# Loading and splitting x by token tiles with whole rows, instead of by column pieces, in a one-core decoder-layer kernel

## The reference, cut to what matters

```python
def _rmsnorm(x, g):
    xf = x.astype(jnp.float32)
    xf = xf * lax.rsqrt(jnp.mean(xf * xf, axis=-1, keepdims=True) + EPS)
    return xf.astype(x.dtype) * g
...
    xn = _rmsnorm(x, n1g)
    z = xn @ w_in
    bg, cg, xt, q, k, v, o, ig, fg = jnp.split(z, _SPLIT_IDX, axis=-1)
```

## Time and profile before

| what | value |
|---|---|
| median of 3 runs | 2495.88 us (2492.79 to 2497.23) |
| the profiled execution's own time | 2492.38 us |
| its span in the profile | 2490.3 us |
| TensorE busy | 2458.9 us (99%) |
| DVE busy | 1771.7 us (71%) |
| ACT busy | 895.0 us (36%) |
| mean granted TensorE clock | 0.997 of full speed |

### The profile page before, as it was taken

How to read it: one execution, slowest core, us unless ns; L and a number is a source line. 1 busy time by engine, 2 the same in 40 slices (tenths; PEclk the granted TensorE clock), 3 DMA queues, 4 the chain that set the end, 5 groups by cost and what they waited for, 6 DMA issues and landing times.

```text
span 2490.3 us, 44310 instructions
## 1 busy us (share of the span) xinstructions
PE 2458.9 (99%) x17632; PEld 2393.4 (96%) x17632; DVE 1771.7 (71%) x2487; ACT 895.0 (36%) x1236; POOL 38.4 (2%) x60
## 2 busy tenths in 40 slices
PE   8999999999999998999999999999999999999998
PEld 8999999999999997999999999999999899999886
DVE  7576575575687668887778777877777866866435
ACT  5212222222133335434343434343444533544313
POOL 0000000000000000000000000000000000000100
PEclk9999999999999999999999999999999999999999
DMA  5433333333235665344343433434333655745722
GB/s 131 99 119 95 84 112 100 89 104 102 86 115 155 186 200 187 111 127 119 102 134 111 128 112 109 127 110 128 100 111 105 250 155 158 266 129 142 274 81 76
DMA packets 458922, 325.54 MB, mean 131 GB/s; under 512 B 14130, under 2 KB 429006, under 8 KB 456368
## 3 DMA queue, kind: packets, MB, share of 16 engines
q1 hardware_dynamic: 403704, 250.29, 34.6%
q10 hardware_dynamic: 51448, 58.42, 7.7%
q0 software_dynamic: 3584, 14.16, 1.5%
HBM read 264.49 MB, written 58.34 MB: 130 GB/s over the span
## 4 chain that ended last, share of the span: by engine, by line
PE 94%; DVE 3%; DMA 2%; ACT 1%; issue 1%; SPq 0%; DVEq 0%; ACTq 0%
PE ps L604 21%; PE ps L844 17%; PE ps L848 17%; PE ps L846 17%; PE ps L607 10%; PE ps L612 3%; PE ps L859 2%; PE ps L952 2%; PE ps L956 2%; PE ps L954 2%; DMA xtok<-in_x_sample_dram 1%; DMA opraw<-hop 0%; PE ps L960 0%; PE ps L961 0%; PE ps L871 0%
## 5 line engine op out<-in xcount | busy, mean ns | idle before, releaser
L844 PE MATMUL ps<-ophi,gw_ring 128*128 128x288 f32 x3248 | 963.2, 297 | 11.7 <-ACT p1c L1291 6.6
L846 PE MATMUL ps<-oplo,gw_ring 128*128 128x288 f32 x3248 | 959.1, 295 | 0.0
L848 PE MATMUL ps<-ophi,gw_ring 128*128 128x288 f32 x3248 | 957.2, 295 | 0.0
L844 PEld LDWEIGHTS ps<-ophi,gw_ring 128*128 128x128 f32 x3248 | 610.1, 188 | 13.6 <-ACT p1c L1291 7.0
L848 PEld LDWEIGHTS ps<-ophi,gw_ring 128*128 128x128 f32 x3248 | 612.7, 189 | 0.0
L846 PEld LDWEIGHTS ps<-oplo,gw_ring 128*128 128x128 f32 x3248 | 610.9, 188 | 0.2
L1017 ACT ACTIVATE whi<-wraw 128x512 fp32r<-128x512 f32 x256 | 160.7, 632 | 597.3 <-PE ps L607 418.5
L604 PE MATMUL ps<-xhi,whi 128*128 128x288 f32 x1536 | 332.6, 298 | 0.0
L607 PE MATMUL ps<-xhi,wlo 128*128 128x288 f32 x1536 | 328.8, 296 | 0.0
L604 PE MATMUL ps<-xlo,whi 128*128 128x288 f32 x1536 | 328.7, 296 | 0.0
L2100 DVE TENSOR_TENSOR gw_ring<-graw_a,gw_ring 128x1024 fp32r<-128x1024 f32 x195 | 238.7, 1224 | 113.4 <-ACT gw_ring L1264 112.8
(11 more groups left out here) (338 smaller groups left out, 2667.6 us busy)
## 6 DMA issues: line engine op xcount, KB each, us to landing
wraw<-in_w_in_dram SPq DMA_DIRECT2D x96, 512.0 KB, 3.9
graw_a<-in_w_ffn_gate_dram SPq DMA_DIRECT2D x59, 512.0 KB, 3.8
graw_a<-in_w_ffn_up_dram SPq DMA_DIRECT2D x59, 512.0 KB, 4.7
graw_a<-in_w_ffn_down_dram SPq DMA_DIRECT2D x42, 512.0 KB, 6.3
wraw<-in_w_out_dram SPq DMA_DIRECT2D x32, 512.0 KB, 4.3
opraw<-hop SPq DMA_DIRECT2D x14, 1152.0 KB, 11.4
graw_b<-in_w_ffn_gate_dram SPq DMA_DIRECT2D x29, 512.0 KB, 3.8
graw_b<-in_w_ffn_up_dram SPq DMA_DIRECT2D x29, 512.0 KB, 4.8
```

The costliest lines, as they stand in the source:

```text
L844: pe.matmul(out, gw_ring[:, slot, 0, k, :], ophi[p][:, k, :], start=start and k == 0, stop=False, skip_group_check=True)
L846: pe.matmul(out, gw_ring[:, slot, 0, k, :], oplo[p][:, k, :], start=False, stop=False, skip_group_check=True)
L848: mm = pe.matmul(out, gw_ring[:, slot, 1, k, :], ophi[p][:, k, :], start=False, stop=k == GK - 1, skip_group_check=True)
```

## The change

SP loads x by token tiles: five DMAs of 96 whole rows of 8 KB, and two for the last tile. TensorE, ACT and DVE go by 12 units (token tile t, half of the columns), each with eight transposes and 128 x 768 elements. The gate products run by halves of the tokens: the first 32 matmuls stand behind the transposes of unit 8, the other 32 behind the last unit. The first two weight quarters are split after units 5 and 7. The squares are whole rows (2048 columns), three token tiles on ACT and three on DVE, after the last unit. There are fewer idle transposes, `gw_lo` counts what `gw_g` counted, and POOL clears `qz` after the squares are summed.

```diff
@@ -97,12 +97,11 @@
     K_FULL = (4, 4, 4, 4)
     assert sum(K_FULL) == KT
     MIX_K = tuple(range(NG, KT)) + tuple(range(NG))
-    X_PIECES = ((0, 2), (2, 2), (4, 4), (8, 4), (12, 4))
+    XU = 2 * XT
+    KU = KT // 2
     SMALLS = 10
-    SQ_ACT = 4
-    IDLE_FIRST, IDLE_X, IDLE_PIECE = 6, 14, (2, 8)
-    X_LAST = {k0 + n - 1: b for b, (k0, n) in enumerate(X_PIECES)}
-    assert sum(n for _, n in X_PIECES) == KT
+    SQ_ACT = 3
+    IDLE_FIRST, IDLE_X = 6, 10
     QS = float(DK) ** -0.5
     GK = KT // 2
     GU = 6
...
@@ -390,12 +389,10 @@
             xp = x_prompt.rearrange("l t d -> (l t) d")
             xs = x_sample.rearrange("b t d -> (b t) d")
             last = TP - (XT - 1) * XTW
-            for b, (k0, n) in enumerate(X_PIECES):
-                c = slice(k0 * P, (k0 + n) * P)
-                sp.dma_start(xtok[:, 0:XT - 1, c],
-                             xp[0:TP - last, c].rearrange("(t p) d -> p t d", p=XTW)).then_inc(tok_in[b], 16)
-                sp.dma_start(xtok[0:last, XT - 1, c], xp[TP - last:TP, c]).then_inc(tok_in[b], 16)
-                sp.dma_start(xtok[last:XTW, XT - 1, c], xs[:, c]).then_inc(tok_in[b], 16)
+            for t in range(XT - 1):
+                sp.dma_start(xtok[:, t, :], xp[t * XTW:(t + 1) * XTW, :]).then_inc(tok_in[t], 16)
+            sp.dma_start(xtok[0:last, XT - 1, :], xp[TP - last:TP, :]).then_inc(tok_in[XT - 1], 16)
+            sp.dma_start(xtok[last:XTW, XT - 1, :], xs[:, :]).then_inc(tok_in[XT - 1], 16)
 
             def head(h, first=False):
                 i = h * TILES_H + 1
...
@@ -624,34 +621,31 @@
             pe.transpose(ps[:, 0, 0:KT], g1_rows[:], ident[0:KT, 0:KT]).then_inc(g1_t, 1)
             idle_work(IDLE_X)
 
-            def gates(k):
-                pe.wait_ge(x_lo, k + 1)
-                for moving in (xhi, xlo):
-                    for a in range(2):
+            def gates(a):
+
+                pe.wait_ge(x_lo, XU // 2 * (a + 1))
+                for k in range(KT):
+                    for moving in (xhi, xlo):
                         mm = pe.matmul(pair(0)[:, a, :], gw[:, k, :], moving[:, 2 * k + a, :],
                                        start=k == 0 and moving is xhi, stop=k == KT - 1 and moving is xlo)
-                if k % 4 == 3:
-                    mm.then_inc(w_used, 1)
-
-            piece = {k0: b for b, (k0, _) in enumerate(X_PIECES)}
-            for k in range(KT):
-                if k >= 3:
-                    pe.wait_ge(x_lo, k - 2)
-                if k in piece:
-                    if 0 < piece[k] < 3:
-                        idle_work(IDLE_PIECE[piece[k] - 1], 2 * (k % 3 + 1))
-                    pe.wait_ge(tok_in[piece[k]], 16 * 3)
-                for t in range(XT):
-                    p0 = 2 * (k % 3 + 1) + t // 3
-                    mm = pe.transpose(ps[:, p0, (t % 3) * XTW:(t % 3 + 1) * XTW],
+                    if k % KU == KU - 1:
+                        mm.then_inc(w_used, 1)
+
+            for n in range(XU):
+                t, kh = n // 2, n % 2
+                if n >= 3:
+                    pe.wait_ge(x_lo, n - 2)
+                if kh == 0:
+                    pe.wait_ge(tok_in[t], 16 if t < XT - 1 else 32)
+                for i in range(KU):
+                    k = kh * KU + i
+                    mm = pe.transpose(ps[:, 2 + 2 * (n % 3) + i // 4, (i % 4) * XTW:(i % 4 + 1) * XTW],
                                       xtok[:, t, k * P:(k + 1) * P], ident[0:XTW, 0:XTW])
                 mm.then_inc(xt_done, 1)
-                if k == 3:
-                    pe.wait_ge(gw_lo, 1)
-                if k >= 3:
-                    gates(k - 3)
-            for k in range(KT - 3, KT):
-                gates(k)
+                if n == XU - 4:
+                    pe.wait_ge(gw_lo, 2)
+                    gates(0)
+            gates(1)
 
             def gates_by_token():
 
...
@@ -1022,29 +1016,29 @@
 
             act.wait_ge(const_ok, 2)
             act.activation(rstd_col[:, 0:1], ident[:, 0:1], ACT.Copy)
-            act.wait_ge(gw_g, 1)
+            act.wait_ge(gw_lo, 1)
             act.activation(gw[:, :, 0:2 * H], gw_raw[:], ACT.Copy).then_inc(gw_hi, 1)
 
-            def square(b, t):
-
-                k0, n = X_PIECES[b]
-                x = xtok[:, t, k0 * P:(k0 + n) * P]
-                act.activation(x, x, ACT.Square, accum_out=ss_part[:, t, b:b + 1]).then_inc(ss_ok, 1)
-
-            squares = []
-            for k in range(KT):
-                p0 = 2 * (k % 3 + 1)
-                act.wait_ge(xt_done, k + 1)
-                act.activation(xhi[:, 2 * k:2 * k + 2, :], ps[:, p0:p0 + 2, 0:HT], ACT.Copy).then_inc(x_hi, 1)
-                if k in X_LAST:
-                    squares += [(X_LAST[k], t) for t in range(SQ_ACT)]
-                if squares:
-                    square(*squares.pop(0))
-                if k in (KT - 4, KT - 2):
-                    q = (k - (KT - 4)) // 2
-                    hi(1, q, gain=q + 1)
-            for b, t in squares:
-                square(b, t)
+            def square(t):
+                x = xtok[:, t, :]
+                act.activation(x, x, ACT.Square, accum_out=ss_part[:, t, 0:1]).then_inc(ss_ok, 1)
+
+            def unit(n):
+
+                t, kh = n // 2, n % 2
+                cols = slice((t % 3) * XTW, (t % 3 + 1) * XTW)
+                own = lambda v: v.rearrange("p (h b k a) t -> p h b k a t", h=2, b=2, a=2)[:, kh, :, :, t // 3, cols]
+                bank = 2 + 2 * (n % 3)
+                return ps[:, bank:bank + 2, 0:4 * XTW].rearrange("p b (k t) -> p b k t", t=XTW), own
+
+            for n in range(XU):
+                src, own = unit(n)
+                act.wait_ge(xt_done, n + 1)
+                act.activation(own(xhi), src, ACT.Copy).then_inc(x_hi, 1)
+                if n in (5, 7):
+                    hi(1, n // 2 - 2, gain=n // 2 - 1)
+            for t in range(SQ_ACT):
+                square(t)
             hi(1, 2, gain=3)
             hi(1, 3, gain=4)
             act.wait_ge(rb_rec, 1)
...
@@ -1500,7 +1494,7 @@
             pool.wait_ge(const_ok, 1)
             pool.affine_select(out=ident[:], in_=ident[:], compare_op=ALU.not_equal, fill=1.0, base=0,
                                pattern=[[-1, P]], channel_multiplier=1).then_inc(const_ok, 1)
-            pool.wait_ge(xt_done, KT)
+            pool.wait_ge(rb_rec, 1)
             pool.memset(qz[:], 0.0).then_inc(const_ok, 1)
 
             def spill(h, j):
...
@@ -1594,29 +1588,32 @@
             dve.wait_ge(tile_read, 1)
             dve.wait_ge(gw_in, 16)
             g1 = vecs[:, V_G1:V_G1 + KT].unsqueeze(2).to_broadcast([P, KT, 2 * H])
-            tt(gw_raw[:], gw_raw[:], g1, ALU.mult).then_inc(gw_g, 1)
+            tt(gw_raw[:], gw_raw[:], g1, ALU.mult).then_inc(gw_lo, 1)
+            dve.wait_ge(gw_lo, 1)
             dve.wait_ge(gw_hi, 1)
             tt(gw[:, :, 2 * H:4 * H], gw_raw[:], gw[:, :, 0:2 * H].bitcast(F32), ALU.subtract).then_inc(gw_lo, 1)
             dve.memset(ssq_c[:], 0.0)
-            def square(b, t):
-                k0, n = X_PIECES[b]
-                x = xtok[:, t, k0 * P:(k0 + n) * P]
-                return stt(x, x, 1.0, x, ALU.mult, ALU.mult, accum_out=ss_part[:, t, b:b + 1])
-
-            squares = []
-            for k in range(KT):
-                p0 = 2 * (k % 3 + 1)
-                dve.wait_ge(x_hi, k + 1)
-                tt(xlo[:, 2 * k:2 * k + 2, :], ps[:, p0:p0 + 2, 0:HT],
-                   xhi[:, 2 * k:2 * k + 2, :].bitcast(F32), ALU.subtract).then_inc(x_lo, 1)
-                if k in X_LAST:
-                    squares += [(X_LAST[k], t) for t in range(SQ_ACT, XT)]
-                if squares and k % 2:
-                    square(*squares.pop(0))
-                if k in (KT - 4, KT - 2):
-                    split(1, (k - (KT - 4)) // 2, V_G1)
-            for b, t in squares:
-                ins = square(b, t)
+
+            def square(t):
+                x = xtok[:, t, :]
+                return stt(x, x, 1.0, x, ALU.mult, ALU.mult, accum_out=ss_part[:, t, 0:1])
+
+            def unit(n):
+
+                t, kh = n // 2, n % 2
+                cols = slice((t % 3) * XTW, (t % 3 + 1) * XTW)
+                own = lambda v: v.rearrange("p (h b k a) t -> p h b k a t", h=2, b=2, a=2)[:, kh, :, :, t // 3, cols]
+                bank = 2 + 2 * (n % 3)
+                return ps[:, bank:bank + 2, 0:4 * XTW].rearrange("p b (k t) -> p b k t", t=XTW), own
+
+            for n in range(XU):
+                src, own = unit(n)
+                dve.wait_ge(x_hi, n + 1)
+                tt(own(xlo), src, own(xhi).bitcast(F32), ALU.subtract).then_inc(x_lo, 1)
+                if n in (5, 7):
+                    split(1, n // 2 - 2, V_G1)
+            for t in range(SQ_ACT, XT):
+                ins = square(t)
             link(ins)
 
             tile_done(0)
```

(16 more changed lines are left out.)

## The result

The changed kernel takes 2512.74 us in the median of 5 runs, beside 2495.3 us (5 runs) for the kernel before on the same chip: ratio 1.0071, 95% interval 1.0059 to 1.0083, some 17.4 us more. The forecast was 2503.7 us and the range ended at 2509. The direction was right; the size, and with it the main cause, were not. The profiled execution took 2512.74 us with a span of 2511.0.

The account below looks back on a forecast made before the run. TensorE was taken to bound the kernel, so only its opening before the first product counts; load 0, moved wait +5.5, squares +1.1 and clock +1.2 gave +7.8 and 2503.7 us, range 2496.5 to 2509.

Parts of the forecast that it names:

- The sum: Total for the opening: load 0, moved wait +5.5, squares +1.1, clock +1.2, together +7.8 us.
- The gates' weights come late: Rival: gw_raw lands only with the last of x, behind 8 KB rows; +5 us more, 2509 us, chance 0.09.
- The load: Loading x to 96 partitions: whole rows instead of pieces leave the rate at 241 GB/s, 0 us.
- W: Landing of the first half of the first weight tile (wraw), queued behind x; claimed to stay at 25.95 us.
- The moved wait: First weight split now stands after unit 5 of 12, so units 6 to 11 wait for W: +5.5 us.
- The way from W to the first product: Time from W to the projection's first product: claimed 13.1 us after the change against 7.6 before.
- The clock: TensorE's gates' second half runs at a lower clock after a gap of about 2 us: +1.2, between 0 and 1.7.
- The squares, +1.1: DVE's three squares after unit 11 delay the copy of zg and lengthen TensorE's wait for rstd: +1.1 us.
- Whole rows load at full speed: Rival: x loads at 417 GB/s and W comes at 17.7 us; -1.6 to +1.2, 2494 to 2497 us, chance 0.15.

Follow-up runs that it names:

- e1: Changed kernel with the gw_raw DMA moved from ScalarE's queue to the head of SP's, ahead of x: 2502.30 us, ratio 1.0032.
- e5: Changed kernel with gw_raw first, 128 rows per tile, first two weight quarters split after the last unit, gates in parts: 2495.31 us, ratio 1.0005.
- b2: Kernel before with x's pieces loaded as 128 rows instead of 96 for each of the first five tiles: 2492.58 us, ratio 0.9996.
- e2: Changed kernel with each 8 KB row of x loaded as four 2 KB pieces, gw_raw still on ACT's queue: 2497.53 us (one run).
- e8: Changed kernel with gw_raw first, 96 rows, weight quarters split after the last unit and gates in parts: 2501.95 us, ratio 1.0028.
- e12: e8 with the squares shared out between ACT and DVE, some of them among the units: 2494.17 us, ratio 1.0004.
- b1: Kernel before with the gw_raw DMA held until the fourth piece of x is in the chip: 2513.44 us, ratio 1.0076.

## Why the prediction was wrong

The step that failed is a landing time left as it was. The sum took gw_raw as there in time, since it lands 5.1 us after its issue and its DMA is untouched by the diff. It appeared only as the rival "The gates' weights come late", with the circumstance named rightly (late behind 8 KB rows) and a chance of 0.09; the argument against it was that "until about 16 us nothing waits for it that doesn't wait for W". It came at 25.3.

The rival was also mis-sized, +5 instead of the 12.0 us by which e1 and after differ. Measured at the first low part of the weights (37.63 in after, 26.17 in e1) the 11.5 us are: 1.3 by which gw_raw is ready later than wraw was in e1 (25.36 against 24.09), 1.6 for its own preparation (priced 1.0), 6.8 for six units (priced 5.3), and 1.8 for the wait of whi for the gates' first half, which the rival left in the load's shadow, where it could no longer be.

The other steps, read in e1, where the gate weights are out of the way:

- The load. "W unmoved at 25.95": the rate was right (247 and 242 against 241 GB/s), W came at 24.1, 1.9 earlier, twice the 1 us that the forecast's own range allowed; why, these views don't show. That the landing on 96 partitions holds the rate down, e5 and b2 bear out. But the way x is cut counts too, which the forecast ruled out: the same tiles in 2 KB pieces came at 283 GB/s, and W at 22.9 (e2).
- The moved wait. Its place is as forecast: six units before, DVE idle 5.39 us released by wraw, six units behind. The way from W to the first product took 15.4 us (24.1 to 39.48) instead of the 13.1 worked out, and of 7.6 before. 1.7 of the excess of 2.3 is the gates' second half, 5.9 instead of 4.2. Most of the rest is the 0.79 us in which the first low part waits for whi (the line at 26.17 in e1): the gates' first half, which the sum had done by then, was still running.
- The clock. That 1.7 is what the forecast gave as its upper bound (+1.2 taken); in after the granted clock is 0.50 from 44 to 48 us. It had fallen behind a gap of 1.19 us (0.53 from 42 to 44), ahead of the gap of 1.89 before the gates.
- The squares, +1.1. Not seen: zg came 0.7 us behind the first product in e1 and 0.8 in after, and the wait for rstd was 0.32 and 0.40 beside 0.36. The slow gates hid them. Their price shows where the gates end early: 4.7 us from the first product to rh between e8 and e12.
- The sum of these, +7.8 us, is the forecast of a kernel in which the gate weights come first, and e1, which is that kernel, takes 2502.30 against 2493.59 us beside it, +8.7. That the two are so close is partly luck. At rh e1 is 5.9 later than before, and the sum is 1.9 too high: W came 1.9 earlier, the squares' 1.1 were not there, and the way took 1.1 more than the 13.1 with the clock's 1.2.

One sum of a rival is off too: in "Whole rows load at full speed" -2.7, +1.1 and 0 to 1.7 make -1.6 to +0.1, not +1.2, so its upper end is 2496.

One thing stays open: how the DMA engines share their turns between two queues is not shown by these views, only that the weights are late beside whole rows and land when x ends. The 2.4 us by which the profiled execution of after is late beyond the 18.0 at rh lie within the scatter: from rh to the end of the span, where no edit changes the work, the profiled executions of this case take 1737 to 1746 us.

## What to carry to other kernels

A transfer that the diff does not touch can still move by 19 us when its neighbours on the DMA engines are cut into other pieces: list every DMA in flight beside the changed one, say who waits for it, and issue small-piece loads that gate the first work ahead on the same queue. When one wait in an in-order engine is taken away and little comes of it, look for the second that holds the same instructions, and then for the work that the delay had been hiding. And price a wait of TensorE with the stretch at the lower clock that can follow it: 3.26 us of waiting lost 5.8 in e5.

## What was unexpected of the hardware

- 2048 pieces of 32 B (gw_raw, 64 KB) landed 3.4 us after their issue ahead of x on the same queue (e1), 5.1 beside pieces of 1 KB, 6.1 beside 2 KB at the start (e2), 8.8 beside 2 KB and smaller pieces in the middle of the load (b1), 20.3 beside 8 KB rows to 128 partitions, 24.0 beside 8 KB rows to 96.
- The Trainium skill (DMA: Bandwidth & Descriptors, "Queues, rings and completion order") has each engine go round between queues and take a packet of some 9 to 17 descriptors at a turn. As an estimate from it, 128 of the 2048 pieces on each of 16 engines take 8 to 15 turns, and x's 36 rows an engine 3 to 4. The weights would then come behind x, and the measured landing, 2.7 us behind it, agrees. By the same estimate the 144 pieces an engine of e2 take 9 to 16 turns, and the weights would come near the end of x; the measured 6.1 us does not agree.
- Reading 736 rows to 128 partitions is faster than reading the 576 that are needed to 96: x ends at 19.3 instead of 22.6.
- The granted clock of an early stretch can read 1.00 while TensorE is slower: in e1 6 to 20 us reads 1.00 while 16 transposes take 2.82 us; in after 16 of them take 1.75 at 39.35 us, inside a stretch of 1.00. And in e1 22 to 24 us reads 1.00 with gates' products 0.24 us apart, as they are in after in the stretch of 0.50. There the spacing of like instructions (0.24 or 0.13 us for a gates' product) is the better witness.
